# Residual, low parts and sums of squares of the stage entries on VectorE alone, with three tiles in their shadow, a third PSUM pair, and the norm row read from PSUM

## The reference, cut to what matters

```python
for layer in range(DEPTH):                       # 2
    h = _rmsnorm(x, pre_mix_g[layer])
    h = mixer(h)                                 # a different one in each layer
    x = x + _rmsnorm(h, post_mix_g[layer])
    h = _swiglu(_rmsnorm(x, pre_ffn_g[layer]), w_gate, w_up, w_down)
    x = x + _rmsnorm(h, post_ffn_g[layer])
...
proj = rmsnorm(x, norm_gain) @ w_in              # the hybrid layer
...
return rmsnorm(x + mixed @ w_out, final_gain)
```

## Time and profile before

| | |
|---|---|
| median of 3 runs | 4799.15 us (4797.67 to 4809.35) |
| the profiled execution | 4806.57 us, its span 4804.8 us |
| granted TensorE clock, mean | 0.922 of full speed |
| PE busy | 4334.1 us, 90% |
| DVE busy | 1906.0 us, 40% |
| ACT busy | 1234.7 us, 26% |
| POOL busy | 1053.2 us, 22% |

### The profile page before, as it was taken

The page is one execution under the profiler, slowest core; times in us unless marked ns, Lnnn a source line. Parts: engine busy times, 40 slices in busy tenths (PEclk is TensorE's granted clock), DMA queues, the critical chain, the costliest instruction groups (busy, mean ns, idle before and its releaser), DMA issues.

```text
span 4804.8 us, 49144 instructions
## 1 busy us (share of the span) xinstructions
PE 4334.1 (90%) x20146; PEld 3418.6 (71%) x20146; DVE 1906.0 (40%) x2436; ACT 1234.7 (26%) x1575; POOL 1053.2 (22%) x508
## 2 busy tenths in 40 slices
PE   7889799999669999879999996898999999999778
PEld 6457588888546666667888875787788887766656
DVE  6742412222442222231222225521656656356552
ACT  3334221111222222332111113222223222144411
POOL 1003322222311111332222223222111111022143
PEclk9999899999769898989999997999999999899898
DMA  2002011111100000101111111222111112032142
GB/s 95 18 14 79 23 51 49 49 49 49 53 31 14 18 18 14 70 27 44 49 49 49 49 49 58 89 101 107 66 51 43 58 53 105 32 116 64 60 158 88
DMA packets 76841, 270.96 MB, mean 56 GB/s; under 512 B 8772, under 2 KB 9416, under 8 KB 72648
## 3 DMA queue, kind: packets, MB, share of 16 engines
q1 hardware_dynamic: 76616, 267.82, 16.5%
HBM read 219.55 MB, written 48.23 MB: 56 GB/s over the span
## 4 chain that ended last, share of the span: by engine, by line
PE 78%; DVE 14%; ACT 3%; POOL 2%; DMA 2%; issue 1%; SPq 0%; DVEq 0%; POOLq 0%; ACTq 0%
PE ps L349 49%; PE ps L378 7%; PE ps L716 2%; PE ps L2051 2%; PE ps L1382 2%; DVE t L482 2%; PE ps L2063 2%; PE ps L1366 2%; PE ps L2059 1%; PE ps L1384 1%; PE ps L3101 1%; PE ps L2104 1%; DMA gb<-g_keep 1%; DVE ps L541 1%; DVE n L3118 1%
## 5 line engine op out<-in xcount | busy, mean ns | idle before, releaser
L295 POOL TENSOR_TENSOR wlo<-wraw,whi 128x1024 fp32r<-128x1024 f32 x301 | 726.3, 2413 | 2814.8 <-ACT whi L287 2806.8
L349 PE MATMUL ps<-xhi,whi 128*128 128x512 f32 x3024 | 991.6, 410 | 128.4 <-DVE xlo L504 90.3
L349 PE MATMUL ps<-xlo,whi 128*128 128x512 f32 x3024 | 958.2, 399 | 0.0
L349 PE MATMUL ps<-xhi,wlo 128*128 128x512 f32 x3024 | 955.4, 398 | 0.0
L287 ACT ACTIVATE whi<-wraw 128x1024 fp32r<-128x1024 f32 x301 | 319.0, 1060 | 2126.6 <-PE ps L349 1812.5
L349 PEld LDWEIGHTS ps<-xhi,whi 128*128 128x128 f32 x3024 | 570.6, 194 | 266.8 <-DVE xlo L504 87.5
L349 PEld LDWEIGHTS ps<-xlo,whi 128*128 128x128 f32 x3024 | 585.5, 194 | 126.7
L349 PEld LDWEIGHTS ps<-xhi,wlo 128*128 128x128 f32 x3024 | 583.4, 193 | 126.2
L541 DVE TENSOR_TENSOR ps<-ps,t 128x1024 f32<-128x1024 f32 x161 | 198.4, 1232 | 1141.8 <-PE ps L349 1137.9
L378 PE MATMUL ps<-xhalf,whi 128*128 128x512 f32 x1024 | 379.3, 453 | 5.6 <-POOL wlo L295 5.6
L349 PE MATMUL ps<-xhalf,whi 128*128 128x512 f32 x1024 | 286.2, 403 | 33.0 <-DVE xhalf L504 21.1
(11 more groups left out here) (488 smaller groups left out, 5158.4 us busy)
## 6 DMA issues: line engine op xcount, KB each, us to landing
wraw<-in_w_dram SPq DMA_DIRECT2D x301, 512.0 KB, 3.6
g_keep<-gates SPq DMA_DIRECT2D x64, 256.0 KB, 2.4
gb<-g_keep SPq DMA_DIRECT2D x32, 512.0 KB, 5.2
p_keep<-stage SPq DMA_DIRECT2D x30, 512.0 KB, 2.9
x<-in_x_dram SPq DMA_DIRECT2D x8, 1024.0 KB, 9.9
x_keep<-x SPq DMA_DIRECT2D x8, 1024.0 KB, 3.9
x<-x_keep SPq DMA_DIRECT2D x4, 1024.0 KB, 7.7
n<-p_keep SPq DMA_DIRECT2D x8, 512.0 KB, 6.6
```

Source lines behind the costliest of these rows:

```text
L295: ge.own().tensor_tensor(K.lo(c), K.raw[:, c % NRAW, :], K.hi(c).bitcast(F32), SUB).then_inc(*K.G(("lo", c)))
L349: done = mm(into[a][:, h, :], wt, x[h], start=(i == 0 and j == 0), stop=(i == n - 1 and j == 2), skip_group_check=True)
```

## The change

- **Work moves.** In the entries VectorE does update, residual, low part and the adding of squares, in a skewed order: the update and the residual of tile i+1 stand ahead of the low part and the add of tile i. POOL has nothing left in the entries. In `mix_out` VectorE adds the squares and copies the result to SBUF, which ACT did; ACT only squares. In the last down product of an ffn and in the tail VectorE adds the squares, which POOL did.
- **Norm row.** The update reads "back" from its two PSUM banks in two halves of 512 positions, without waiting for ACT's copy, and the copy is gone there.
- **Three tiles.** Ring P has a third pair (4, 5), ring Q is left with banks 6 and 7, and pair 2 is lent to Q within the mixers and the tail. Every entry now multiplies three tiles together (`wide_tensor`): for mixer1 the gates and two tiles of p0, for an ffn both gate tiles and one of the next gate product, for the hybrid layer the two small ones and one projection.
- **Sum.** The sum is complete before its columns are read, so only one set of 16 narrow matmuls is left (`columns_tensor`); in the entries it stands ahead of the last step's products. ACT squares the last tile before it makes its high part, and splits its next chunk after tile 5.

```diff
-def stat_tensor(pe, K, n, acc, sq, last):
-    mm = pe.e.matmul
-    b = take(pe, K, K.Q, n, "sum")
-    pe.wait_ge(*K.at(n, "add"))
-    for i in range(8):
-        mm(K.ps[:, b, i:i + 1], acc[:, part(i)], K.ones[:, 0:1], start=(i == 0), stop=False, skip_group_check=True)
-    pe.wait_ge(*K.at(n, "sq", last))
-    for i in range(8):
-        d = mm(K.ps[:, b, i:i + 1], sq[:, part(i)], K.ones[:, 0:1], start=False, stop=(i == 7), skip_group_check=True)
-    d.then_inc(*K.T((n, "sum")))
...
+def wide_tensor(pe, K, tiles, xs):
+    n = len(xs)
+    bases = [K.reserve("main", n) for _ in tiles]
+    pairs = [take(pe, K, K.P, key, m) for key, m in tiles]
+    for i, (xhi, xlo, events) in enumerate(xs):
+        for ev in events:
+            pe.wait_ge(*K.at(*ev))
+        for (key, m), base, b in zip(tiles, bases, pairs):
+            c, o = divmod(pe.block, 8)
+            pe.block += 1
+            K.order.append(("main", base + i))
+            pe.wait_ge(*K.at("lo", c))
+            done = block_products(...)
...
 def enter_vector(ve, K, N):
     def update(i):
         for ev in Y.ready(i):
             ve.wait_ge(*K.at(*ev))
-        ve.own().scalar_tensor_tensor(out=Y.out[:, i, :], in0=Y.out[:, i, :], scalar=Y.gain(i), in1=Y.scale, op0=MUL, op1=MUL).then_inc(*K.V((n, "y", i)))
+        for h in range(2):
+            y = Y.out[:, i, HALVES[h]]
+            ve.wait_ge(*K.at(Y.stat, "back", h))
+            ve.own().scalar_tensor_tensor(out=y, in0=y, scalar=Y.gain(i), in1=K.bank(Y.stat, "back", h), op0=MUL, op1=MUL).then_inc(*K.V(("free", (Y.stat, "back", h))))
+    def residual(i):
+        if Y.before_x is not None:
+            ve.wait_ge(*K.at(*Y.before_x, i))
+        ve.own().tensor_tensor(X[:, i, :], X[:, i, :], Y.out[:, i, :], ADD).then_inc(*K.V((n, "x", i)))
...
+    if Y is not None:
+        update(0)
+        residual(0)
+        update(1)
+    low(0)
+    if Y is not None:
+        residual(1)
+    for i in range(1, 7):
         if Y is not None:
-            ge.wait_ge(*K.at(n, "y", i))
-            if Y.before_x is not None:
-                ge.wait_ge(*K.at(*Y.before_x, i))
-            ge.own().tensor_tensor(X[:, i, :], X[:, i, :], Y.out[:, i, :], ADD).then_inc(*K.G((n, "x", i)))
+            update(i + 1)
+            residual(i + 1)
+        low(i)
+        add(i)
+    add(7)
+    low(7)
+
+def entry_tensor(pe, K, N, tiles):
+    product = wide_tensor(pe, K, tiles, N.xs)
+    for _ in range(7):
+        next(product)
+    columns_tensor(pe, K, N.name, N.acc)
+    next(product)
+    stat_back_tensor(pe, K, N.name, N.sq[0])
...
 def mix_out_vector(ve, K, O):
+    for m in range(8):
+        ve.wait_ge(*K.at("tile", n, m))
+        ve.wait_ge(*K.at(n, "sq", m))
+        if m:
+            square_add(ve, K, n, O.ysq[:, :], O.sq[m % 2][:, :], m)
+        ve.own().tensor_copy(O.out[:, m, :]..., K.pair(n, m)).then_inc(*K.V((n, "o", m), ("free", (n, m))))
...
-    enter_gpsimd(ge, K, S.N1)
     ffn_gpsimd(ge, K, S.F0)
...
-        K.P, K.Q = K.ring([0, 1]), K.ring([4, 5, 6, 7])
+        K.P, K.Q = K.ring([0, 1, 2]), K.ring([6, 7])
```

More of the change, by code:

```diff
@@ L2 @@
 from contextlib import ExitStack
+from itertools import chain
 import numpy as np
@@ L300, in nothing, with wide_walk, walk @@
     pass
-def walk(seat, K, make, n, m_tiles, wide=1):
-    m = 0
+def wide_walk(seat, K, make, n, w):
+    make(seat, K, seat.block // 8)
+    for _ in range(n):
+        for _ in range(w):
+            seat.block += 1
+            if seat.block % 8 == 0:
+                make(seat, K, seat.block // 8 + 1)
+        yield
+def walk(seat, K, make, n, m_tiles, wide=1, first=0):
+    m = first
     while m < m_tiles:
@@ L345, in dense_tensor @@
                 pe.wait_ge(*K.at("lo", c))
[L346 to L350, removed]
+                done = block_products(pe, K, into[a], xhi, xlo, K.hi(c)[:, part(o)], K.lo(c)[:, part(o)], i == 0, i == n - 1)
                 events_now = [("chunk", c)] * (o == 7) + [("tile", key, m + a)] * (i == n - 1)
@@ L466, in enter_scalar, with high, square, square_add @@
     n, X = N.name, N.X
+    def high(i):
+        for hi, lo, x in N.H.parts(i, X[:, i, :]):
+            se.own().activation(hi, x, ACT.Copy, scale=N.gain(i)).then_inc(*K.S((n, "high", i)))
+    def square(i):
+        if i > 2:
+            se.wait_ge(*K.at(n, "add", i - 2))
+        se.own().activation(N.sq[i % 2] if i else N.acc[:, :], X[:, i, :], ACT.Square).then_inc(*K.S((n, "sq", i)))
     for i in range(8):
         se.wait_ge(*K.at(n, "x", i))
[L469 to L472, removed]
-        else:
[L474 to L482, removed]
+        if i < 7:
+            high(i)
+            square(i)
+        else:
+            square(i)
+            high(i)
+        if i == 5:
+            weights_scalar(se, K, se.block // 8 + 2)
+def square_add(ve, K, n, acc, sq, i):
+    ve.wait_ge(*K.at(n, "sq", i))
+    ve.own().tensor_tensor(acc, acc, sq, ADD).then_inc(*K.V((n, "add", i), (n, "add")))
 def enter_vector(ve, K, N):
@@ L1076, in ffn_order, with ffn_first, gate_steps @@
     return order
+def ffn_first(n):
+    return [((n, "gate", 0), 0), ((n, "gate", 0), 1), ((n, "gate", 1), 0)]
+def gate_steps(seat, K, make, i):
+    if i == 0:
+        return iter(range(2))
+    return chain(range(int(i == 1)), walk(seat, K, make, 8, 2, first=int(i == 1)))
 def ffn_tensor(pe, K, F):
@@ L1266, in gate_rows_scalar, with project_steps @@
     yield
+def project_steps(seat, K, make, j):
+    first = 0 if j else 2
+    return chain(range(first), walk(seat, K, make, 8, 4, first=first))
 def project_tensor(pe, K, M, j):
@@ L1278, in turn @@
         d.then_inc(*K.T(("turned", j, v)))
-    for m in dense_tensor(pe, K, ("p", j), M.N.xs, 4):
+    for m in chain(range(0 if j else 2), dense_tensor(pe, K, ("p", j), M.N.xs, 4, first=0 if j else 2)):
         if m is not None and m >= 2:
```

231 lines of the change are left out of this document (100 added, 131 removed).

## The result

The changed kernel takes 4735.9 us (median of 4 runs, 4732.93 to 4739.91) against 4798.41 before; the ratio is 0.9866, with a 95% interval of 0.9849 to 0.9883. So it is faster by 62.5 us (1.3%), where 79 were forecast; 4735.9 lies within the range on record and 16 us above its middle. The profiled execution took 4739.91 us, with a span of 4738.1; the one before had 4806.57.

A forecast was written before the change was run, and what follows sets the result against it. PE's work, plus its waits and lower-clock stretches, was taken as the bound, with the entries bound by DVE. Terms summed to -79.3 us, 4806.6 to 4727.3 profiled, 4720 us median (-1.65%); eight-in-ten range 4682 to 4758.

The forecast's parts named there:

- Term 1: Entries e1 to e4, from mean to last low part: about 44.6 us against 52.5, -31.5 us over the four.
- Term 2: Behind an entry's last low part, stall included: -14.2 us in two ffn, -10.6 in mixer1, -3.0 in the hybrid layer.
- The stall: PE stands at an entry's seventeenth block until 2.4 us after the last low part, idle 8 to 10 us, awaiting POOL's `wlo`.
- Term 3: Ends of the two ffn: mean 9.5 us behind PE's end instead of 15.0, -5.5 each, -11 us in all.
- The bound from above: Ends of ffn: with two `wlo` locks on VectorE's adds, only -3 us at each end.
- Term 4: Two mix_out: third pair removes a PE wait and slow start, -5.0; later mean +2.5; -2.5 each, -5 us.
- Term 5: mixer0: pow chain hidden, two waits become one, -4 us; 0 if the convolution on VectorE doesn't let it through.
- Term 6: Tail: adds to VectorE, one narrow set less, one add later in line; 0 us (0 to +1.3).
- A: Third chunk in e1 to e4: no stall, POOL's wait met earlier; 51 us less in all, 4669 us; chance 8%.
- B: Four entries: VectorE's two-input operations stay near 3.4 us, adding 131 us, 4851 us; chance 4%.
- C: Chains on VectorE and stage ends absorb the entries' gain; time within 0.3% of no change; chance 3%.
- D: Entries and stage ends: two `wlo` locks, no mixer0 gain, PE falling behind; -35 to -55 left, 4744 to 4764 us; 15%.

## Why the prediction was right, and where it was off

Measured on the two profiles, 66.7 us, against 79.3 forecast.

- **Term 1, mean to last low part, -31.5 forecast, -19.1 measured** (4.6, 4.9, 4.6, 4.9). This is the step that failed: the sum of VectorE's instructions, "8 x (1.42 + 1.26 + 1.32) + 7 x 1.25 = 40.75", and "so 3.83 after the mean". Its own sign, 44 to 45 us behind the mean (e4 47), was missed: 47.7 to 48.0 (e4 49.7). In e2 the first update starts 4.67 behind the mean, and the instructions take 43.0. The 0.84 at the start is a wait that the sum left out: by the program the update stands behind VectorE's fence at the end of f0, which waits for all eight transposes, so reading the row by halves brings nothing there. ACT's copy, which is ahead of such a fence, started 1.15 behind the first transpose in the run that reads the row from SBUF. Half of the other 2.2 is the half update: 0.75, not 0.69. L822, one PSUM operand in and the same size, was taken as the nearest row, but it has a constant where the update has a column `vec`; the nearest row was the half low part in the earlier trace rows, three in 2.42. The other half is some 0.1 us of gaps around each low part. That every two-input operation would fall to 1.22, the reason of the term, is right: all 32 residuals are at 1.224 to 1.227, and with the residual back on POOL the 3.40 is there again. By the Trainium skill ("SBUF — State Buffer", the section on the two separate sides) the one that starts first holds the shared ports; the trace agrees, POOL 0.06 us ahead in that run.
- **Term 2, behind the last low part: -14.2, -10.6 and -3.0 forecast.** The stall is where it was put and as long (10.5 to 11.3 us of idle PE in all four entries), and its removal gave 45.6 of 45, though 36.4 of it in the entries. From L7 to PE's last block f0 is shorter by 8.3 and f1 by 4.8, forecast 7.1 each. mixer1: broadcast at 86.7 behind the low part, forecast 87.7, so -11.6. Hybrid, up to the first norm of the scans: -7.0, 4 more than forecast; why is open.
- **Term 3, ends of ffn: -11 forecast, -7.6 measured.** "One `wlo`" was two: both of the last splits fall on adds of VectorE (3.34, 3.00), and each pushes accumulation and add back. The bound from above was used too little; POOL's adds, which the change removed, were the better choice with one set of narrow matmuls.
- **Term 4, mix_out: -5 forecast.** In o0 PE's end came 4.5 earlier and the mean 2.5 later behind it, so -2.0 of -2.5. In the second one it can't be told from the heads ahead of it; together they are at -6.2.
- **Term 5, mixer0: -4 forecast, -5.0 measured** at the norm of the convolution.
- **Term 6, tail: 0 to +1.3 forecast.** From the first norm of the scans on the changed kernel is 5 us *longer* (1334.5 to 1329.4), of which 1.6 is the last add. The rest is in code that nobody touched, and two executions of the changed kernel differ there by 3.4.

The missing 12.6 us are those of terms 1, 3 and 6 (12.4, 3.4, 5), against 8 us gained more than forecast in the hybrid layer, the heads and mixer0. That the total missed by no more is in part luck: 21 us stand against 8, and of the 8 no cause is shown. Of the rivals, A (no stall) is what the early split then made true by an edit: 4690 rather than its 4669, as its other terms carry the same errors. B (two-input operations stay slow) is excluded by every entry, C (absorbed) by the interval of the ratio. Of D, the two splits beside adds at each end of an ffn came; its PE falling behind in the entry didn't come: in e2 PE is at full clock from 1272.50 on, 5 us after its first block in the entry, and then waits for low parts.

Open: what sets the clock's rises in the heads, scans and tail. The runs show 5 to 17 us between kernels that differ in nothing there. Differences of a whole time below that size aren't evidence about an edit, and are read from the stretch of the edit in the trace.

## What to carry to other kernels

Before a stage gets more work in its shadow, count for how many chunks the weights are ready when it starts, and look at what the next chunk's producer stands behind: here a fence turned the third tile into a loss of 10 to 24 us, and splitting that chunk ahead of it gave 45. Work that goes from POOL to VectorE is worth it where both run two-input operations on SBUF side by side, and not where VectorE's instruction reads PSUM and POOL keeps up. Price an instruction by a row of the same size and the same operands, the scalar's kind included. Look for fences not only behind a change but ahead of it: one here made an earlier start impossible.

## What the runs showed of the hardware that was not expected

- PE can be busy without a gap and stay at half clock for long: 29.00 of 29 us busy, clock 0.59, with rows at 1.05 us for 24 us of it, behind transposes and small matmuls of mixer1. The same program did it again in a second execution, and 2.7 us of delay shortened it.
- Behind one and the same wait of 3.64 us PE went on at half clock in one run (two matmuls in 1.05) and at full clock in another (0.62), after some 650 us in which PE's rows had the same length in both.
- A column of 128 values as the scalar of SCALAR_TENSOR_TENSOR takes 0.06 us more than a constant, at 128x512: 0.748 to 0.752 against 0.691 to 0.693.
- Two updates of 128x512 take 1.50 to 1.53 us, one of 128x1024 takes 1.28, with the second operand in PSUM or in SBUF alike (0.748 and 0.752). By the Trainium skill ("Perfetto Trace Analysis", Optimizing Scalar/DVE Operations) an instruction has a fixed cost of access, larger for PSUM; the first part agrees (0.22 us for each, by these numbers: twice 0.752 less 1.28), a difference between PSUM and SBUF isn't seen here.
